# Level sums of gated linear attention on one core: each product streams 64 of its 128 token columns

## The reference

```python
bc = jnp.cumsum(to_chunks(log_a), axis=3)
diff = bi[:, :, :, None, :] - bi[:, :, None, :, :]
decay = jnp.exp(jnp.where(causal, diff, -jnp.inf))
att = jnp.einsum('bhtd,bhsd,bhtsd->bhts', qi, ki, decay)
intra = jnp.einsum('bhts,bhse->bhte', att, vi)
```

## Time and profile before

| | |
|---|---|
| median of 3 runs | 1985.93 us (1984.94 to 1986.22) |
| span of the profiled execution | 1983.6 us |
| median of the runs less that span | 2.3 us |
| busy: TensorE matmul, TensorE weight load | 1903.8 us, 1582.0 us |
| busy: VectorE, ACT, POOL | 987.2, 629.1, 297.2 us |
| GLA phase with its tail | about 600 to 1015 us |
| mean granted TensorE clock | 0.991 |

### The profile page before, as it was taken

How to read it: one execution, slowest core, us unless ns; L and a number is a source line. 1 busy time by engine, 2 the same in 40 slices (tenths; PEclk the granted TensorE clock), 3 DMA queues, 4 the chain that set the end, 5 groups by cost and what they waited for, 6 DMA issues and landing times. The chain is left out here.

```text
span 1983.6 us, 26324 instructions
## 1 busy us (share of the span) xinstructions
PE 1903.8 (96%) x9008; PEld 1582.0 (80%) x9008; DVE 987.2 (50%) x1779; ACT 629.1 (32%) x1219; POOL 297.2 (15%) x475
## 2 busy tenths in 40 slices
PE   6999999999999899999979999999999999999999
PEld 4888778788787778878868888788888888888887
DVE  6542743743736748484765555533233323433343
ACT  5343333332334344444452123421212121212210
POOL 2211311212305433333411000000000000000000
PEclk9999999999999899999999999999999999999999
DMA  5111222112122111110235232111111111111112
GB/s 144 49 62 52 65 69 82 48 58 86 43 69 71 33 33 54 32 53 26 79 106 185 81 95 85 36 50 42 53 53 42 42 53 53 52 32 53 53 42 85
DMA packets 141501, 123.98 MB, mean 63 GB/s; under 512 B 6160, under 2 KB 125232, under 8 KB 140928
## 3 DMA queue, kind: packets, MB, share of 16 engines
q1 hardware_dynamic: 129808, 90.25, 14.9%
q0 software_dynamic: 7024, 24.62, 3.8%
q10 hardware_dynamic: 4608, 8.39, 1.1%
HBM read 105.27 MB, written 17.97 MB: 62 GB/s over the span
## 5 line engine op out<-in xcount | busy, mean ns | idle before, releaser
L1414 PE MATMUL bank<-act_hi,w_hi 128*128 128x512 f32 x1792 | 711.1, 397 | 4.2 <-DVE act_lo L1313 3.6
L1416 PE MATMUL bank<-act_hi,w_lo 128*128 128x512 f32 x1792 | 699.6, 390 | 0.0
L1415 PE MATMUL bank<-act_lo,w_hi 128*128 128x512 f32 x1792 | 698.8, 390 | 0.0
L1414 PEld LDWEIGHTS bank<-act_hi,w_hi 128*128 128x128 f32 x1792 | 337.4, 188 | 74.3 <-DVE act_lo L1313 4.5
L1416 PEld LDWEIGHTS bank<-act_hi,w_lo 128*128 128x128 f32 x1792 | 337.1, 188 | 71.6
L1415 PEld LDWEIGHTS bank<-act_lo,w_hi 128*128 128x128 f32 x1792 | 337.6, 188 | 67.3
L995 DVE TENSOR_TENSOR w_lo<-w_raw,w_hi 128x1024 fp32r<-128x1024 f32 x150 | 184.6, 1234 | 275.1 <-ACT w_hi L646 275.1
L646 ACT CAST w_hi<-w_raw 128x1024 fp32r<-128x1024 f32 x150 | 156.5, 1047 | 252.5 <-PE bank L1416 251.4
L946 ACT CAST y_hi<-yf 128x512 fp32r<-128x512 f32 x60 | 37.2, 621 | 285.4 <-DVE yf L1403 211.7
L1359 DVE TENSOR_TENSOR xk<-lvl_ps,xk 128x512 f32<-128x512 f32 x120 | 82.4, 690 | 60.5 <-PE lvl_ps L1416 60.5
L1359 DVE TENSOR_TENSOR xk<-bank,xk 128x512 f32<-128x512 f32 x120 | 82.8, 690 | 57.4 <-PE bank L1416 57.3
(11 more groups left out here) (218 smaller groups left out, 2346.7 us busy)
## 6 DMA issues: line engine op xcount, KB each, us to landing
w_raw<-in_w_in SPq DMA_DIRECT2D x60, 512.0 KB, 3.6
w_raw<-in_w_ffn_gate SPq DMA_DIRECT2D x22, 512.0 KB, 3.7
w_raw<-in_w_ffn_up SPq DMA_DIRECT2D x22, 512.0 KB, 3.7
w_raw<-in_w_ffn_down SPq DMA_DIRECT2D x22, 512.0 KB, 3.2
gate_scratch<-gbuf ACTq DMA_DIRECT2D x32, 256.0 KB, 2.1
gl<-gate_scratch POOLq DMA_DIRECT2D x16, 512.0 KB, 4.6
wb<-weight_scratch POOLq DMA_DIRECT2D x4, 1536.0 KB, 6.7
xin<-in_x SPq DMA_DIRECT2D x8, 512.0 KB, 8.3
```

Source lines behind the costliest of these rows:

```text
L1414: pe.matmul(ps, lhs_hi, rhs_hi, start=first, stop=False)
L1415: pe.matmul(ps, lhs_hi, rhs_lo, start=False, stop=False)
L1416: return pe.matmul(ps, lhs_lo, rhs_hi, start=False, stop=last)
```

## The change

The second operand of each level product is no longer the whole tile but only the columns of the intervals' second halves (64 of 128 in every level, in 64/m runs of m columns), and the result goes to the same columns of the level's tile in PSUM. The stationary operand stays the whole tile. The other 64 columns are then never written, so VectorE clears both banks once, ahead of the first head of phase 2. The product of line 1610, the mask and the sum are as before. The line numbers of the diff are those of the kernel before, and of the one after.

```diff
@@ -1192,6 +1192,8 @@
             dve_head_a(h, True)
         leave_phase(dve)
         enter_phase(dve, 2)
+        for b in range(2):
+            dve.memset(lvl_ps[:, b, :], 0.0)
 
 
         def dve_head(h, tail):
@@ -1604,8 +1606,11 @@
                     pe.wait_ge(st_evac, base + 3 + c // 4)
                 pe.wait_ge(l_mask, 2 * n)
                 for lv in range(7):
+                    m = 64 >> lv
                     t = fbuf[:, p % 2, lv, cols]
-                    pe.matmul(lvl_ps[:, lv // 4, P * (lv % 4):P * (lv % 4) + P], t, t, start=True, stop=True)
+                    late, o = (v.rearrange("p (n two m) -> p n two m", two=2, m=m)[:, :, 1, :] for v in
+                               (t, lvl_ps[:, lv // 4, P * (lv % 4):P * (lv % 4) + P]))
+                    pe.matmul(o, t, late, start=True, stop=True)
                 ct = slice(P * c, P * c + P)
                 pe.matmul(lvl_ps[:, 1, 3 * P:4 * P], kf[:, ct], qf[:, ct], start=True, stop=True
                           ).then_inc(l_ready, 1)
```

## The result

The changed kernel takes 1988.41 us (median of 20 runs, 1985.28 to 1991.11) against 1985.31 us (20 runs, 1983.10 to 1987.01) of the kernel before, measured beside it. The ratio is 1.0015, with a 95% interval of 1.0009 to 1.0022: **3.1 us slower**, small but clear. The profiled execution has a span of 1987.6 us against 1983.6.

A forecast was written before the change was run, and what follows sets the result against it. TensorE, busy 96% of the span, was taken as the bound, with weight loads as long as the matmuls. Terms -0.9 + 0 + 0 us on 1985.9 gave 1985.0 us, range 1981 to 1990.5 us.

The forecast's parts named there:

- the allowance for low-clock stretches: Whole kernel: one low-clock stretch more or less moves the time by another 1.5 us or so.
- Part 1, the seven products: Level products on TensorE: weight loads keep pairs near 111 ns apart, 2 ns gained per pair, -0.9 us.
- Rival A: Level products: loads are not a limit, distance falls to 56 ns, 24.6 us gained, 1961 us; 4% for the whole.
- the half way: Level products: loads run somewhat faster, half way between 56 and 111 ns, 12 us gained, 1973 us; chance 5%.
- Two lesser signs: Profile after, TensorE: a single matmul record gets shorter, and the busy total may drop with no change in span.
- Parts 2 and 3, spaced reads and writes: Six spaced levels on TensorE: reads taken at nothing, bounds 0 and +2.3 us; PSUM writes with gaps bounded by nothing.
- Rival B: Spaced PSUM writes are slow: last level's pairs last 230 ns, 7.6 us lost, 1992.6 us; chance 7%.
- Part 4, the clears: Two VectorE clears behind the phase barrier: 1.2 us, hidden in idle time, cost on the end 0, at most +0.3 us.
- Part 6, the clock: TensorE's clock at the blocks: fewer columns might add a low-clock stretch; one block cost 1.35 us more; none taken.
- Rival C: Three or more added low-clock stretches, about 1.35 us a block, cost over 4 us, to about 1990; chance 3%.

The follow-up runs named there:

- dense streams: The changed kernel, but every level streams the chunk's last 64 columns in one dense run, also written densely: 1987.60 us, ratio 1.0010 to the kernel before.
- trimmed version: The kernel before with the clears, level 0 as one 64 by 64 product and level 1 as two of 32 by 32: 1989.08 us, ratio 1.0020.

## Why the prediction was wrong

The kernel moved the other way: +3.1 us, where -0.9 was forecast, with an interval of the measurement that excludes no change. That 1988.4 us still lies within 1981 to 1990.5 is luck as far as the sum goes: the allowance for low-clock stretches covers it.

- **Part 1, the seven products: the mechanism was right.** The distance is 111 ns before and after, and with a load of 64 columns it is 58 ns. The -0.9 us was too much: the steady distance stayed, so the term is 0. Rival A is refuted, the half way as well: pairs with a load of 128 columns stay at 111 ns. Two lesser signs didn't come either. The record of a matmul did not get shorter (median 275 ns), and TensorE's busy total rose by 9.9 us.
- **Parts 2 and 3, spaced reads and writes:** taken at nothing, and nothing is seen at a full clock but the 3 ns of the last levels, hidden behind the load. The dense streams lose about as much as the spaced ones. Rival B is refuted. Its ground was weak as well: "A spaced column costs about twice a dense one" was read from the earlier trace rows, but line 1498 at 287.56 us takes its stationary operand with gaps too. Its last weight loads have records of 0.34 us where the dense ones have 0.19, and start 0.24 us apart. That 0.23 us may be the load's, and the row says nothing certain of the stream.
- **Part 4, the clears:** right. 1.02 us against the 1.2 I took, hidden, and 1.0001 alone.
- **Part 6, the clock, is the step that failed:** "Fewer columns per block might add such a stretch; I take none". There the term was put at nothing without a reason. In the profile the change adds three low stretches of 3.4 to 6.8 us at narrow blocks and lengthens one at 640 us. Blocks made wide again beside idle time (1.0001) and idle time filled (1.0006, clock 0.991) take the added stretches away. Rival C had this mechanism, at 3%. What I held against it was that "from 700 us on, the clock stays at 1.00 although TensorE idles before several blocks". That was read from blocks with wide products, and says nothing of narrow ones. Each added stretch cost 0.8 to 1.2 us of delay net, near the 1.35 us a block of the rival. At its peak the delay was up to 2 us more; that part went as waits vanished.

## What to carry to other kernels

The small f32 matmul here was paid by the longer of its stream and its weight load. Find the load's own distance in a block that starts after idle time before halving the stream. If the stream was not the only limit, halving it leaves TensorE half the columns for the same time, and here that brought the clock down beside idle time: treat such a cut as a risk, not as free, and look at the granted clock around every wait. A cut of the load paid with 14 loads of one width in a row; with six small ones ahead of ten wide ones it lost.

## What the runs showed of the hardware

- The low clock needed both the idle time and the narrow block here. A wait of 1.65 us before a wide block left the clock at 1.00; before a narrow one it fell in most executions, to judge by the mean clock (16 of 20 runs at 0.988 or below, the kernel before never under 0.991 in 80). In the profile the fall comes 0.3 to 1.2 us after the narrow block has begun. Either remedy, wide blocks or filled idle time, kept it up. In the one profile of the trimmed version, blocks with only two of seven levels cut down had it lowered, too.
- The Trainium skill, "TensorE: Matmul & The Clock Gate", section "LDWEIGHTS (loading the stationary operand)", gives a load's time as proportional to its columns, an estimated 107 ns for 128 and 53 ns for 64. The trace comes close for f32 by the distance of the starts, 111 and 58 ns; the record of one load lasts 192 and 138 ns.
- Where the width of the weight load changes, time is lost: 0.33 us of idle before the first of 14 narrow loads, and the same before the first of six. Of 0.75 us that the smaller loads save in a block, 0.34 us went there and behind it.
- The runs of one program differ in their mean clock, and their time goes with it. Grouped by mean clock, the changed kernel runs from 1985.9 us (0.990 and 0.991) to 1989.5 us (0.986 and 0.987).
